# Token tile 1 before the samples in the later norms, its first two query blocks projected alone

## The chip, the cores and the metric

The kernel runs on one core of one Trainium2 chip, in one launch. The metric is the device time of that launch in microseconds (us), the median of three executions. All arithmetic is fp32.

## The reference

One layer of a decoder trunk, for 512 prompt tokens and 8 sample tokens of width 1024. The first half (windowed attention, gated DeltaNet, two gates, an output projection) yields `x`. The second half is a retrieval of single experts, and it is the stage that the change touches:

```python
mix = merged @ p['w_out']
x = x + gt1 * _rmsnorm(mix, p['g_post_mix'])
h2 = _rmsnorm(x, p['g_pre_ffn']) * (1.0 + sc2) + sh2
# _peer(h2, w_query, sub_keys, expert_u, expert_v), for each token and each of 8 heads:
qry = (xb @ w_query)                     # 16 blocks of 128 columns, two for each head
s = einsum(qry, sub_keys)                # two score rows of 128 keys for each head
sv, si = top_k(s, 16)                    # then the best 16 of the 16 x 16 sums
u, v = expert_u[eidx], expert_v[eidx]    # 16 rows of each, 1024 wide
out += (gate * gelu(xb . u)) * v
x = x + gt2 * _rmsnorm(out, p['g_post_ffn'])
```

## The kernel before

**Tiles and units.** The tokens are four tiles of 128 (t = 0 to 3) and the 8 samples (t = NT = 4). The expert stage is a list of 33 units (tile, head), eight for each tile and one for the samples. A unit of a token tile has 8 ticks, and there are 260 ticks. In each tick GpSimd issues two gathers (L480), each of 128 rows of 2048 floats (an expert's u and v side by side, 1.05 MB) into a ring of 7 slots. So tick i owns gathers 2i and 2i + 1, and units change at ticks 8, 16, 24 and so on. Tile 1 begins at tick 64.

**The ring.** For each gather VectorE makes a dot product with the tile's activations (L2390), ScalarE applies Gelu (L890) and makes a diagonal of weights (L892), and TensorE multiplies by the v half into `fsum` or `dbank` (L1648, L1654) and frees the slot. GpSimd may issue gather n only when TensorE is done with gather n - 7. Every engine works through its own program in order.

**What is woven in.** While tile 0's units run, the engines also finish the first half for the later tiles, and this work stands at fixed ticks, in tables written by hand: the remaining gates (`GATE_AT`), tile 0's query blocks (`FIRST_AT`), the output projection of the later tiles in four quarters e of three ticks each (`MIX_FROM`, `mixes_at`), the two norms (`NORMAL`, `SECOND`), the transposition of `h2` (`TURN`), then the 16 query blocks of all later tiles and the samples (`QUERY`, TOK - P = 392 columns at once). `SPREAD` broadcasts vectors of the modulation over the partitions. The keys of these tables are ticks. `LATER` says in which order tiles go through mixes, norms and TURN. In `woven(i)` TensorE issues what belongs to tick i, after the tick's two expert products; ScalarE empties the PSUM banks of tick i after the Gelus of tick i + 1; VectorE does its share at the end of tick i. Most of the woven products go through two PSUM banks (`abank0`, `abank1`) in turn.

**A query block.** It is 8 matmuls over `h2T[1]`, half of them before the first expert product of the next tick (`query_begin`) and half behind it (`query_end`). TensorE first waits until `h2T_ready` is NT + 1 = 5: tile 0, the samples and tiles 1 to 3 are all turned. ScalarE counts `h2T_ready` up at the end of each `turned`. Scores for the first head of tile 1 need blocks 0 and 1 (`scores(1, "first")`), and VectorE searches them at the end of tick 55, behind a wait for `first_sc`. The weights of a block (512 KB) come by SyncE's queue into four places; the load of a block waits until the block four before it has been used.

**The full rows of h2.** `second_part(t, None)` on VectorE rewrites tile t's `h2` for the dot products, at the ticks in `ROWS_LATER`, behind a wait for `h2T_ready`. In the kernel before tile 1's waits only for its own turn (3), tile 2's for 4, tile 3's for 5.

## Time and profile before

| | |
|---|---|
| median of 3 executions | 1865.48 us (1865.09 to 1865.55) |
| the profiled execution | 1861.27 us, its span 1859.5 us |
| TensorE | 1447.3 us busy, 78% of the span |
| VectorE, ScalarE, GpSimd | 67%, 38%, 33% |
| bytes moved | 647.54 MB, 348 GB/s over the span |

The table of the page divides the span into 40 slices of 46.5 us. The first gather is issued at 461.9 us; from slice 11 on (465 us) the DMA engines are nearly always busy and carry most of the time. In slices 15 to 20 the rate falls below that of the slices around them. A share of busy time is a mean over the whole span, and stages with different limits lie in it.

### The profile page before, as it was taken

To read this page: it belongs to the slowest core of one execution; us is meant where nothing else is said; L and a number is where in the kernel's file an instruction comes from. 1 tells how busy PE (TensorE), PEld (TensorE's weight loads), DVE (VectorE), ACT (ScalarE), POOL (GpSimd) and SP (SyncE) were. 2 spreads that over 40 slices of the span, in tenths; PEclk is the share of its full clock that TensorE was granted. 3 is DMA by queue.
4 is the path that set the end of the run, shared out by engine and by line. 5 is a ranking of instruction groups with operands and counts; after the bars stand their busy time and mean duration, and the time that the engine had idled before them with its cause. 6 is when DMAs were issued, how large, how long until landed. Compare 5 with 4: busy or idle time off the path is not lost.

```text
span 1859.5 us, 23227 instructions
## 1 busy us (share of the span) xinstructions
PE 1447.3 (78%) x8298; PEld 684.0 (37%) x8298; DVE 1248.9 (67%) x2827; ACT 704.1 (38%) x1799; POOL 611.3 (33%) x590
## 2 busy tenths in 40 slices
PE   8999988999888889689776666666666676667666
PEld 4777877887454446444222111101111110001001
DVE  3077678776866665776767666777667677667665
ACT  3145472213545553935324222432222243222223
POOL 1100000000543323333445444454444444444442
PEclk9999998999999999899988767867766676665666
DMA  9533362126999999999999999999999999999997
GB/s 348 179 121 118 129 241 80 35 80 219 417 421 419 422 414 405 401 342 394 413 420 423 425 424 424 425 424 425 424 424 423 421 423 417 422 421 418 423 422 305
DMA packets 101059, 647.54 MB, mean 348 GB/s; under 512 B 11858, under 2 KB 12026, under 8 KB 32933
## 3 DMA queue, kind: packets, MB, share of 16 engines
q0 software_dynamic: 76912, 555.82, 72.3%
q1 hardware_dynamic: 23840, 90.16, 13.3%
q8 instruction: 66, 1.08, 0.2%
q14 instruction: 49, 0.40, 0.1%
q10 hardware_dynamic: 192, 0.09, 0.0%
HBM read 640.84 MB, written 6.18 MB: 348 GB/s over the span
## 4 chain that ended last, share of the span: by engine, by line
PE 38%; DMA 38%; DVE 9%; ACT 9%; issue 5%; POOL 1%; ACTq 0%; SPq 0%; DVEq 0%; POOLq 0%
DMA arena<-in_euv,consts 37%; PE abank L926 23%; PE dbank L1654 4%; PE dbank L926 4%; DVE arena L2390 3%; PE fsum L1654 2%; PE fsum L1648 2%; ACT consts L892 2%; ACT L890 2%; ACT small L890 1%; ACT L795 1%; DMA arena<-in_wstream 1%; PE fsum L990 1%; POOL arena L480 1%; PE abank L1538 1%
## 5 line engine op out<-in xcount | busy, mean ns | idle before, releaser
L2390 DVE CUSTOM_DVE_ANT_0 arena<-arena 128x1024 f32<-128x1024 f32 x520 | 632.8, 1223 | 387.6 <-DMA arena<-in_euv,consts 386.7
L480 POOL DMA_INDIRECT arena<-in_euv,consts x520 | 577.0, 1110 | 784.3 <-PE dbank L1654 335.5
L926 PE MATMUL abank<-arena 128*128 128x128 f32 (+4 forms) x2456 | 555.1, 383 | 19.5 <-ACT arena L497 6.9
L1654 PE MATMUL dbank<-arena,consts 128*32 128x512 f32 x1024 | 364.5, 850 | 202.2 <-ACT consts L892 201.9
L926 PEld LDWEIGHTS abank<-arena 128*128 128x128 f32 (+1 forms) x2456 | 393.0, 191 | 176.0 <-issue 65.4
L890 ACT ACTIVATE small<-small 128x1 f32<-128x1 f32 x520 | 104.7, 201 | 639.5 <-DVE small L2390 632.9
L1654 PE MATMUL fsum<-arena,consts 128*32 128x512 f32 x512 | 191.2, 873 | 113.9 <-ACT consts L892 113.3
L1654 PEld LDWEIGHTS dbank<-arena,consts 128*32 128x32 f32 x1024 | 42.4, 124 | 487.9 <-ACT consts L892 475.9
L497 ACT ACTIVATE arena<-abank 128x512 f32<-128x512 f32 (+5 forms) x237 | 116.0, 489 | 253.2 <-PE abank L926 240.0
L892 ACT ACTIVATE consts<-arena,small 128x32 f32<-128x32 f32 x520 | 167.1, 321 | 16.9
L1654 PEld LDWEIGHTS fsum<-arena,consts 128*32 128x32 f32 x512 | 21.6, 126 | 263.5 <-ACT consts L892 261.0
L1648 PE MATMUL fsum<-arena,consts 128*32 128x256 f32 x1024 | 77.3, 410 | 41.1 <-ACT consts L892 40.9
L926 PE MATMUL dbank<-arena 128*128 128x128 f32 (+6 forms) x544 | 79.7, 315 | 0.4 <-DVEq L1817 0.4
L890 ACT ACT_TABLE_LOAD x57 | 73.1, 1283 | 4.2 <-DVE small L2390 1.8
L926 PEld LDWEIGHTS dbank<-arena 128*128 128x128 f32 (+2 forms) x544 | 67.0, 201 | 9.6 <-issue 4.6
L1648 PEld LDWEIGHTS fsum<-arena,consts 128*32 128x32 f32 x1024 | 25.1, 112 | 89.5 <-ACT consts L892 59.1
L459 POOL DMA_DIRECT2D out_deltas<-arena x1 | 0.5, 539 | 145.4 <-DVEq L2020 145.4
L497 ACT ACT_TABLE_LOAD x27 | 34.6, 1283 | 22.8 <-PE abank L926 21.7
L2390 DVE DVE_READ_ACCUMULATOR2_ANT small<- 128x1 f32 x520 | 42.8, 82 | 0.0
L795 ACT ACT_TABLE_LOAD x32 | 41.1, 1283 | 1.5
L2256 DVE MAX8 arena<-arena 128x8 f32<-128x128 f32 (+3 forms) x99 | 30.0, 331 | 15.7 <-ACTq L780 7.7
L1553 PE MATMUL abank<-arena,consts 128*32 128x512 f32 x256 | 39.6, 692 | 0.9 <-ACT arena L773 0.9
(338 smaller groups left out, 1196.1 us busy)
## 6 DMA issues: line engine op xcount, KB each, us to landing
arena<-in_wstream SPq DMA_DIRECT2D x140, 512.0 KB, 6.2
arena<-in_euv,consts POOLq DMA_INDIRECT x520, 13.2
arena<-in_wout SPq DMA_DIRECT2D x8, 1024.0 KB, 8.8
arena<-in_x SPq DMA_DIRECT2D x5, 512.0 KB, 6.8
arena<-in_sdel POOLq DMA_DIRECT2D x1, 2048.0 KB, 9.1
out_deltas<-arena POOLq DMA_DIRECT2D x1, 2048.0 KB, 12.0
out_yp<-arena SPq DMA_DIRECT2D x4, 512.0 KB
arena<-mod SPq DMA_DIRECT2D x3, 512.0 KB, 10.0
```

The costliest lines, as they stand in the source:

```text
L480: pool.indirect_dma_start(ring[n % SLOTS], None, I["euv"], bass.IndirectOffsetOnAxis(cur[:, u % 2, c:c + 1], 0)).then_inc(ring_in[n % SLOT ...
L497: step(A(dst, src, func, **kw), s.aring_free)
L795: A(gexp[r, :], best[r, :], ACT.Exp, bias=nbest[r, :], accum_out=gsum[r, :]).then_inc(s.gexp_ready, 1)
L890: step(A(gel[:, q % 2, place:place + 1], dot[:, q % 2, place:place + 1], ACT.Gelu), s.gelu_done)
L892: A(S[:, q % 2, place, :], E4g[:, u % 2, c0:c0 + 32], ACT.Copy, scale=gel[:, q % 2, place:place + 1]).then_inc(s.diag_ready, 1)
L926: return pe.matmul(out, lhsT, rhs, start=first, stop=last)
L990: last = pe.matmul(mod_bank[0][32 * j:32 * j + NCOND, half * 256:half * 256 + 256], cT[:, at_, :], w[:, j * 256:(j + 1) * 256], start=at_ ...
L1553: last = pe.matmul(b[32 * k:32 * k + 32, :], ident[:, 32 * j:32 * j + 32], h2_all[t][:, g * 512:(g + 1) * 512], start=True, stop=True, ski ...
L1648: last = pe.matmul(out[bank][32 * strip:32 * strip + 32, 256 * (e % 2):256 * (e % 2) + 256], weighed, v, start=first, stop=h == PH - 1 and ...
L1654: last = pe.matmul(out[e][to:to + 32, :], weighed, v, start=h == 0 and kk == 0, stop=h == PH - 1 and kk == 3, skip_group_check=True)
L2256: did(key, dve.max(val[:, 0:8], src))
L2390: TTR(uh, uh, rep[j] if t < NT else h2sb, 1.0, 0.0, ALU.mult, ALU.add, dot[:, n // NQ % 2, n % NQ:n % NQ + 1]).then_inc(s.dots_done, 1)
```

## The change

Tile 1 goes first through mixes, norms and TURN. `MIX_FROM` is one tick later, and with it all mixes; the gates from the tenth on stand up to one tick later and tile 0's last query block one tick sooner. The norms and turns are two ticks later. The first two query blocks of tile 1 alone (128 columns) are projected at ticks 51 and 52 (`ALONE`); their other 264 columns follow at ticks 76 and 79, for which their weights are loaded a second time. The other blocks run from tick 54 on. The last `SPREAD` moves from tick 56 to tick 63.

```diff
-        LATER = [NT, 1, 2, 3]
+        LATER = [1, NT, 2, 3]
...
-        MIX_FROM = 34
+        MIX_FROM = 35
...
-        NORMAL = {45: 0, 46: 1, 47: 2, 48: 3}
-        SECOND = {47: 0, 48: 1, 49: 2, 50: 3}
-        TURN = {48: 0, 49: 1, 50: 2, 51: 3}
-        ROWS_LATER = {53: 1, 55: 2, 57: 3}
-        QUERY_AT = (52, 53, 54, 55, 57, 58, 59, 62, 64, 67, 70, 73, 76, 79, 82, 85)
...
+        NORMAL = {47: 0, 48: 1, 49: 2, 50: 3}
+        SECOND = {49: 0, 50: 1, 51: 2, 52: 3}
+        TURN = {50: 0, 51: 1, 52: 2, 53: 3}
+        ROWS_LATER = {54: 1, 56: 2, 58: 3}
+        ALONE = {51: 0, 52: 1}
+        QUERY_AT = (54, 55, 57, 58, 59, 62, 65, 68, 71, 74, 76, 79, 83, 86, 89, 92)
+        QUERY = dict(zip(QUERY_AT, list(range(2, 12)) + [0, 1] + list(range(12, 2 * PH))))
...
-        SPREAD = {36: (0, 1), 39: (2, 3), 42: (4, 5), 44: (8,), 56: (6, 7)}
+        SPREAD = {37: (0, 1), 40: (2, 3), 43: (4, 5), 47: (8,), 63: (6, 7)}
...
+                if i in ALONE:
+                    pe.wait_ge(s.h2T_ready, 2)
+                    project(h2T[1], ((0, P),))
...
+                lo = P if m < 2 else 0
...
-            for n in range(N_AGAIN + 4, N_AGAIN + B_QRY):
+            for n in range(N_AGAIN + 4, N_AGAIN + B_QRY + 2):
...
                 if i in ROWS_LATER:
-                    dve.wait_ge(s.h2T_ready, ROWS_LATER[i] + 2)
+                    dve.wait_ge(s.h2T_ready, NT + 1)
                     second_part(ROWS_LATER[i], None)
```

TensorE around the last turn. In the kernel before: the turn of tile 3 (four matmuls for each half), tick 52's expert products, and then query block 0 on 392 columns.

```order
L926 MATMUL abank<-arena 128x128 [waits aring_free,h2_ready]
L926 MATMUL abank<-arena 128x128 x3
L926 MATMUL abank<-arena 128x128 [waits aring_free]
L926 MATMUL abank<-arena 128x128 x3
L1648 MATMUL fsum<-arena,consts 32x256 [waits diag_ready]
L1648 MATMUL fsum<-arena,consts 32x256 x3
L1648 MATMUL fsum<-arena,consts 32x256 [waits diag_ready]
L1648 MATMUL fsum<-arena,consts 32x256 x3
L926 MATMUL abank<-arena 128x392 [waits aring_free,w_full0,h2T_ready]
L926 MATMUL abank<-arena 128x392 x3
```

And in the changed kernel, from the second block alone (tick 52) to the turn of tile 3 (tick 53):

```order
L932 MATMUL abank<-arena 128x128 [waits aring_free,w_full1,h2T_ready]
L932 MATMUL abank<-arena 128x128 x7
L1665 MATMUL fsum<-arena,consts 32x256 [waits diag_ready]
L1665 MATMUL fsum<-arena,consts 32x256 x3
L1665 MATMUL fsum<-arena,consts 32x256 [waits diag_ready]
L1665 MATMUL fsum<-arena,consts 32x256 x3
L932 MATMUL abank<-skt,arena 128x128 [waits aring_free,qry_ready]
L932 MATMUL abank<-skt,arena 128x128
L932 MATMUL abank<-arena 128x128 [waits aring_free,h2_ready]
L932 MATMUL abank<-arena 128x128 x3
L932 MATMUL abank<-arena 128x128 [waits aring_free]
L932 MATMUL abank<-arena 128x128 x3
```

The blocks of 128 columns and the first scores (from `skt`) now stand ahead of the last turn, and the first block of 392 columns comes two ticks later than before.

VectorE at ticks 53 to 55. The pairs on L2390 are the dot products of the ring, L2172 and L2173 the full rows of tile 1, and L2256 the search of tile 1's first scores. Before:

```order
L2330 TENSOR_TENSOR arena<-consts 128x512 [waits diag_ready,egs_ready]
L2172 SCALAR_TENSOR_TENSOR arena<-arena,small 128x1024 [waits h2T_ready]
L2173 TENSOR_TENSOR arena<-arena 128x1024 [waits dve_step]
L2390 ISA arena,small<-arena 128x1024 [waits ring_in3,h2_ready]
L2390 ISA small 128x1
L2390 ISA arena,small<-arena 128x1024 [waits ring_in4]
L2390 ISA small 128x1
L2390 ISA arena,small<-arena 128x1024 [waits ring_in5]
L2390 ISA small 128x1
L2390 ISA arena,small<-arena 128x1024 [waits ring_in6]
L2390 ISA small 128x1
L2256 MAX arena<-arena 128x8 [waits eg_ready,first_sc]
```

In the changed kernel:

```order
L2347 TENSOR_TENSOR arena<-consts 128x512 [waits diag_ready,egs_ready]
L2407 ISA arena,small<-arena 128x1024 [waits ring_in3]
L2407 ISA small 128x1
L2407 ISA arena,small<-arena 128x1024 [waits ring_in4]
L2407 ISA small 128x1
L2189 SCALAR_TENSOR_TENSOR arena<-arena,small 128x1024 [waits h2T_ready]
L2190 TENSOR_TENSOR arena<-arena 128x1024 [waits dve_step]
L2407 ISA arena,small<-arena 128x1024 [waits ring_in5,h2_ready]
L2407 ISA small 128x1
L2407 ISA arena,small<-arena 128x1024 [waits ring_in6]
L2407 ISA small 128x1
L2273 MAX arena<-arena 128x8 [waits eg_ready,first_sc]
```

Tile 1's rows moved behind the dot products of tick 54, and their wait is now for the value 5, which comes with the turn of tile 3. The search stays at tick 55.

ScalarE in the second norms. Each row on L675 is a sum of squares, followed by a table load and a square root. Before, around `NORMAL`'s last tile, with the samples' turn (128x8x8) between the root and the next Gelu:

```order
L675 ACTIVATE arena,small<-arena 128x1024
L676 ACT_TABLE_LOAD
L676 ACTIVATE small<-small 128x1
L497 ACTIVATE arena<-abank 128x8x8
L890 ACT_TABLE_LOAD
L890 ACTIVATE small<-small 128x1
L892 ACTIVATE consts<-arena,small 128x32
```

In the changed kernel at the same place (128x128 x8 is the turn of tile 1):

```order
L677 ACTIVATE arena,small<-arena 128x1024
L678 ACT_TABLE_LOAD
L678 ACTIVATE small<-small 128x1
L764 ACTIVATE arena<-abank,small 128x128 x8
L896 ACT_TABLE_LOAD
L896 ACTIVATE small<-small 128x1
L898 ACTIVATE consts<-arena,small 128x32
```

The turn of tile 1 now shares a tick with the last of the norms.

## Rows read from the trace of the kernel before

**Rows 1.** The page: the span, the rate in its 40 slices, the chain.

```profile
span 1859.5 us, 23227 instructions
...
GB/s 348 179 121 118 129 241 80 35 80 219 417 421 419 422 414 405 401 342 394 413 420 423 425 424 424 425 424 425 424 424 423 421 423 417 422 421 418 423 422 305
...
PE 38%; DMA 38%; DVE 9%; ACT 9%; issue 5%; POOL 1%; ACTq 0%; SPq 0%; DVEq 0%; POOLq 0%
```

**Rows 2.** Windows: start:end, length, busy us of each engine, PEclk, DMA share, GB/s.

```profile
680.00:740.00 60.00, 52.30 (x515) 39.43 (x516) 34.25 (x86) 22.64 (x69) 20.34 (x19) 0.91 0.99 402
740.00:795.00 55.00, 35.22 (x368) 23.63 (x367) 40.01 (x66) 50.76 (x110) 21.66 (x21) 0.84 1.00 406
795.00:850.00 55.00, 51.10 (x264) 25.11 (x264) 40.23 (x106) 17.29 (x55) 17.36 (x16) 0.94 0.91 343
850.00:900.00 50.00, 42.47 (x272) 17.59 (x272) 34.21 (x82) 29.86 (x78) 21.60 (x20) 0.93 0.99 403
900.00:1000.00 100.00, 76.43 (x374) 28.39 (x368) 64.49 (x160) 31.68 (x103) 45.56 (x43) 0.95 1.01 419
1000.00:1400.00 400.00, 259.25 (x1080) 47.41 (x1080) 282.36 (x695) 128.03 (x392) 182.42 (x171) 0.72 1.01 424
```

**Rows 3.** Two windows inside 795:850, same columns.

```profile
820.00:830.00 10.00, 7.16 (x36) 3.94 (x28) 9.38 (x22) 5.45 (x12) 1.89 (x2) 0.90 0.95 376
830.00:840.00 10.00, 10.00 (x46) 4.43 (x48) 9.93 (x32) 1.77 (x6) 3.18 (x3) 0.76 0.63 226
```

**Rows 4.** Waits from 790 to 870 us: total us, times, longest.

```profile
POOL arena L480 <- PE fsum L1648: 46.3, 19, 6.7
...
DVE arena L2256 <- ACTq L780: 7.7, 1, 7.7
```

**Rows 5.** Timeline of TensorE: start us, length us, what, idle before it.

```profile
708.53 3.72 PE L926 MATMUL abank<-arena 128*128 128x256 f32 x16
...
790.79 1.16 PE L926 MATMUL abank<-arena 128*128 128x128 f32 x8 [0.74 <-ACT arena L762]
...
795.74 2.90 PE L926 MATMUL abank<-arena 128*128 128x392 f32 x8 [2.79 <-ACTq L764]
798.57 0.64 PE L1648 MATMUL fsum<-arena,consts 128*32 128x256 f32 x8
...
828.41 2.07 PE L926 MATMUL abank<-onehot,consts 16*128 16x256 f32 x4 [2.57 <-ACT arena L497]
...
832.28 4.16 PE L926 MATMUL abank<-arena 128*128 128x392 f32 x8
...
846.92 0.64 PE L1648 MATMUL fsum<-arena,consts 128*32 128x256 f32 x8
```

**Rows 6.** Timeline of ScalarE, same columns.

```profile
791.77 3.88 ACT L762 ACTIVATE arena<-abank,small 128x128 f32<-128x128 f32 x8
795.76 0.20 ACT L890 ACTIVATE small<-small 128x1 f32<-128x1 f32 x1
796.00 0.32 ACT L892 ACTIVATE consts<-arena,small 128x32 f32<-128x32 f32 x1
...
825.79 1.28 ACT L890 ACT_TABLE_LOAD   x1
```

**Rows 7.** ScalarE's groups from 740 to 800 us: count, busy us, mean ns.

```profile
L676 ACT ACT_TABLE_LOAD x6 | 7.7, 1283 | 0.1
```

**Rows 8.** Timeline of VectorE: a dot, the full rows, the search.

```profile
795.36 1.22 DVE L2173 TENSOR_TENSOR arena<-arena 128x1024 f32<-128x1024 f32 x1
...
799.68 1.23 DVE L2390 CUSTOM_DVE_ANT_0 arena<-arena 128x1024 f32<-128x1024 f32 x1 [0.69 <-DMA arena<-in_euv,consts]
...
811.06 0.49 DVE L2256 MAX8 arena<-arena 128x8 f32<-128x128 f32 x2 [7.68 <-ACTq L780]
```

**Rows 9.** DMA issues: KB of each, median us to landing.

```profile
arena<-in_wstream SPq DMA_DIRECT2D x140, 512.0 KB, 6.2
arena<-in_euv,consts POOLq DMA_INDIRECT x520, 13.2
```

More of the change, by code:

```diff
@@ L330, in scores_at @@
                 return 0, FIRST_AT[i - 1] // 4
-            if QUERY.get(i - 1) == 1:
+            if ALONE.get(i - 1) == 1:
                 return 1, "first"
@@ L337, in scores_at @@
             return None
+        SCORED = [(0, 0), (0, 1)] + [x for x in map(scores_at, range(len(TICKS))) if x and x[1] != "first"]
         LATE = unit_of(1, 0)
@@ L846, in woven @@
                     turned(LATER[TURN[i]])
+                if i in ALONE:
+                    empty(qryL[0][:, ALONE[i], 0:P], slice(0, P))
+                    act.sem_inc(s.qry_ready, 1)
                 if i in QUERY:
@@ L1488, in first_query, with asked_at, query_begin @@
                 project(h2T[0], ((0, P),))
+            def asked_at(t, m):
+                if t == 0 or t == 1 and m < 2:
+                    return m + 1 + (2 * PH if t else 0)
+                return 2 * PH + 3 + list(QUERY.values()).index(m)
             begun = [None, None]
-            def query_begin():
+            def query_begin(m):
+                lo = P if m < 2 else 0
                 w, b = weights(), aring.to_fill()
                 for k in range(KT // 2):
-                    last = mm(b[:, 0:TOK - P], w[:, k, :], h2T[1][:, k, :], k == 0, False)
+                    last = mm(b[:, lo:TOK - P], w[:, k, :], h2T[1][:, k, lo:], k == 0, False)
                     if k == 0:
@@ L1498, in query_begin, with query_end @@
                 begun[0], begun[1] = w, b
-            def query_end():
+            def query_end(m):
+                lo = P if m < 2 else 0
                 w, b = begun
                 for k in range(KT // 2, KT):
-                    last = mm(b[:, 0:TOK - P], w[:, k, :], h2T[1][:, k, :], False, k == KT - 1)
+                    last = mm(b[:, lo:TOK - P], w[:, k, :], h2T[1][:, k, lo:], False, k == KT - 1)
                 last.then_inc(s.aring_full, 1)
@@ L1516, in scores @@
                 g = 0 if g == "first" else g
-                pe.wait_ge(s.qry_ready, 4 * g + max(part) + 1 + (2 * PH if t else 0))
+                pe.wait_ge(s.qry_ready, max(asked_at(t, 4 * g + x) for x in part))
                 b = aring.to_fill()
@@ L1591, in woven @@
                     turned(LATER[TURN[i]])
+                if i in ALONE:
+                    pe.wait_ge(s.h2T_ready, 2)
+                    project(h2T[1], ((0, P),))
                 if i in QUERY:
                     pe.wait_ge(s.h2T_ready, NT + 1)
-                    query_begin()
+                    query_begin(QUERY[i])
                     if replicated(i):
-                        query_end()
+                        query_end(QUERY[i])
                 if replicated(i):
```

19 lines of the change are left out of this document (9 added, 10 removed).

## The prediction

> **What bounds the kernel now.** I read the page first. The chain that ended last is shared equally by TensorE and DMA, 38% each, and the row of rates says where each rules: from slice 21 on the rate stands near 424 GB/s, in slices 14 to 20 it falls to 342 to 414 [rows 1]. So the kernel is bound by bytes wherever the ring is kept fed, and time can be won only where the DMA engines run below 424 GB/s, or by moving fewer bytes. I then cut that part into windows and turned each rate into idle DMA time, length x (424 - rate) / 424: 3.1 us in 680:740, 2.3 in 740:795, 10.5 in 795:850, 2.5 in 850:900, 1.2 in 900:1000 and none in 1000:1400 [rows 2]. That is 19.6 us, over half of it in 55 us, and there TensorE is 93% busy (51.1 of 55). At 740:795 it is ScalarE instead, 50.8 of 55.
>
> Third, I counted gathers in the timelines to put ticks on these times (the dot at 799.68 us is number 110, the first of tick 55). 795:850 holds ticks 53 to 59, and so the query blocks 0 to 6. Half a block takes 2.90 us and the next product starts 2.83 behind it; two halves and two products come to 6.8 us for a tick [rows 5]. The bytes of such a tick need less: a gather has 1.05 MB, 2.47 us at 424 GB/s, a block 0.52 MB, 1.24 us [rows 9], together 6.2 us. TensorE therefore paces the ring, GpSimd waits for it 19 times, 46.3 us in all [rows 4], and ever fewer gathers are in flight. The deepest dip comes behind one event: at 828.41 TensorE has waited 2.57 us for ScalarE, the clock is granted at 0.76 over the next window, which is a stretch at 1.2 GHz and the rest at 2.4, half a block takes 4.16 us instead of 2.90, and the rate is 226 GB/s [rows 3, 5]. In the same ten ticks VectorE waits 7.7 us for the first scores [rows 4, 8], but the indices of tile 1 are not late; it costs only what it holds back of the ring.
>
> **The change, part by part.** *Bytes.* Two blocks are loaded twice: 2 x 1.24 = **+2.5 us**, in a stretch where DMA is the bound and nothing covers it. All other loads only move.
>
> *Start.* Everything from the mixes on stands one tick later, so one more tick of gathers goes ahead of it: 2 x 2.47 = 4.9 us later on the clock, with the same bytes moved per tick, no gain and no loss. Gates move by at most a tick in a stretch with hardly any idle time: nothing.
>
> *Norms, ticks 44 to 54.* ScalarE's list grows. Before, the last mean of the mixes and the first of the second norms fell into the same tick and shared one pair of table loads; now they are in two ticks: 2 x 1.28 = 2.6 us [rows 7]. The stretch has one more tick, with two Gelus and two diagonals at 0.20 + 0.32 each [rows 6], 1.0 us. Emptying two banks of 128 columns and the first scores' bank I put at 0.9 us, from 0.3 us each. Together +4.5 us, so the end of the last turn, at 791.77 + 3.88 = 795.65 us before [rows 6], comes 9.4 us later, but with gather 109 used and not 105. TensorE has room for the two blocks alone (2.3 us each, twice the 1.16 us of 8 records [rows 5]), since it is idle for 20 of 55 us there [rows 2]. In bytes this stretch needs 4 gathers and 2 blocks more, 12.4 us, against 9.4 us of time: about 0.8 us of its 2.3 us of idle DMA is filled, the rest of the difference makes the ring shallower.
>
> The Trainium skill would have this dearer: its page "ScalarE: Activation LUTs", section "What ACT_TABLE_LOAD costs", gives 1283 ns for a load plus about 1380 ns of drain, so 5.3 us for the added pair. The trace agrees with the first part, 1283 ns [rows 7], and not with the second: six loads have 0.1 us of idle time ahead of them together. By the page the sum below would be up to 2.7 us worse.
>
> *Queries, from the last turn to the product of gather 119 (tick 59).* Before: 795.65 to 846.92 + 0.64 = 847.56, 51.9 us [rows 5, 6]. Now blocks 2 to 5 stand in between and not 0 to 5 with part of 6. I lay out the new order with the durations of before. VectorE now waits at tick 54 for the last turn (value 5). Behind that wait stand the full rows of tile 1, the dots of tick 55 and the search; ScalarE's Gelus and TensorE's product 110 wait for those. Two passes at 1.22, a dot at 1.23, Gelu and diagonal 0.5: product 110 can start 4.2 us behind the turn [rows 6, 8]. TensorE has half a block to do meanwhile, 2.9 us, so it loses 1.3. Then: 8 halves at 2.83 = 22.7, 10 products at 0.57 = 5.7, scores and selection 1.1. At tick 57 ScalarE still has the exponential of tile 1's first unit, with two table loads, ahead of its Gelus, and I let the 2.57 us wait stand, and the slow clock behind it: a product and a half block at half speed, 2.2 us. The sum is 1.3 + 22.7 + 5.7 + 1.1 + 2.6 + 2.2 = 35.6 us, 16.3 less than before. With the turn 9.4 us later, product 119 ends **6.9 us sooner**, with the same gathers and blocks fetched. This much idle DMA time is filled at least by TensorE's pace. It can be more, as the ring is fuller at that point: in those 35.6 us DMA could bring 12 gathers and 5 blocks, 35.8 us, so it would hardly stop. The ends are 4 us (the first 1.3 us grows to 4 when gather 110 is late) and 12.8 us (all of 740:850). I take 7.8, with the 0.8 of above in it, since the layout by rows is the nearer of the two.
>
> *Behind it.* The last SPREAD goes from tick 56 to 63, where the scores use a bank too: three banks in one tick, of which TensorE has two, as in tick 56 before. At tick 63 TensorE was late and ScalarE ahead, so I take 1.0 us for its two products and not the dip; the ends are 0 and 5.8 us (the idle time of both windows [rows 3]). The other columns of blocks 0 and 1, at ticks 76 and 79: 264 columns take about the 3.72 us of 256 [rows 5], where a tick has room; ticks with a block at 900:1000 leave 1.2 us idle for six blocks, so two more 0.3 us.
>
> **Sum.** +2.5 - 7.8 + 1.0 + 0.3 = **-4.0 us**. The profiled execution, 1861.27 us with a span of 1859.5 [rows 1], would come to 1857.3. It lies 4.2 us under the median of the runs, so the same difference put on the median gives 1865.48 - 4.0 = **1861.5 us**. A measurement of this kernel tells about 0.2%, 3.7 us, from no change; the forecast lies at that edge.
>
> **The rivals.** *A, the ring stays fed.* With both blocks out of the way, in-flight gathers never run out, and of the 12.8 us nearly all is filled: -12 + 2.5 + 1.3 = -8 us, 1857 us. For it: the byte count of 35.8 against 35.6 us. Against it: the wait of 2.6 us and the slow clock are still in the order.
>
> *B, the new wait gives it back.* VectorE's wait for the value 5 holds the dots of ticks 55 and 56 until ScalarE has done the last turn, and the ring, shallower now, empties there as it did behind the wait of 7.7 us [rows 8]. The gain falls to 4: -4 + 3.8 = about 0, 1865.5 us. For it: in the old order the last turn was behind VectorE's dots of tick 53 only for tile 3's rows, and there was slack; now there is none. Against it: TensorE waits for the same turn anyway.
>
> *C, slower: the spread at the tile's change.* At tick 63 TensorE needs a third bank, which ScalarE empties only after the Gelus of tick 64, and these wait for the first dots of tile 1. If TensorE stands still there, the clock falls for the replicas and the block that follow. Price: a second dip like that of 820:840, 5.8 us, while the first stays where it is (tick 57) and eats 3.9 of the 7.8: +2.5 - 3.9 + 5.8 + 0.3 = +4.7, 1870.2 us. It decides once TensorE idles over 2.5 us at tick 63 or 64. Against it: in the old order ScalarE had emptied ahead of TensorE at this tick.
>
> *D, the stretch isn't paced by the blocks:* only the second load counts, +2.5 us, 1868. The windows speak against it.
>
> **The numbers.** The forecast 0.40, A 0.17, B 0.23, C 0.12, D 0.08. The forecast's own range is 1859.5 to 1864, so it is half above and half below the bound of 3.7 us. Faster by over 0.2%: 0.22 of the forecast, A, and a little of B's low side, 0.42. Slower by over 0.2%: C and some of D, 0.14. Within: 0.44. The range runs from A's lower half to D, 1856.5 to 1868.5, and leaves out C and the tail of A.
>
> **What would show it.** Right: the product of gather 119 ends near 841 us, the window 795:850 carries 370 to 400 GB/s, the turn of tile 3 ends near 805 us, 1.28 us loads stay two to a tick of the norms, and the row of rates is flat at 424 from 900 us on with two more blocks in it. Wrong: a wait of VectorE for ScalarE over 6 us at tick 54 with a rate under 300 behind it (B); TensorE idle over 2.5 us near tick 64 (C); slices 17 and 18 unchanged (D). A turn that ends later than 808 us would make the prediction too low, since all behind it hangs on its time.

## The result, and the profile after

The changed kernel takes 1877.38 us (8 runs), the kernel before 1864.57 us beside it: ratio 1.0071, 95% interval 1.0052 to 1.0089, 13.2 us slower (0.0071 x 1864.57). The forecast was 4 us faster. A second set of runs (c0 below) gave 1.0091 (1.0065 to 1.0116). Its page, of an execution of 1877.11 us, with the rows that answer to [rows 1]:

```profile
span 1875.3 us, 23300 instructions
...
GB/s 360 167 131 105 126 263 54 35 108 234 420 421 420 421 398 382 362 343 384 372 422 422 423 424 425 424 424 425 422 424 424 419 416 408 424 424 424 418 424 314
DMA packets 101348, 648.59 MB, mean 346 GB/s; under 512 B 11891, under 2 KB 12059, under 8 KB 33222
...
PE 42%; DMA 32%; DVE 9%; ACT 9%; issue 5%; POOL 1%; another core or an unknown queue 1%; ACTq 0%; SPq 0%; DVEq 0%; POOLq 0%
```

The chain that ended last leans more on TensorE now (42%, 38% before) and less on DMA (32%, 38% before). The windows of [rows 2], now:

```profile
680.00:740.00 60.00, 53.06 (x501) 37.60 (x500) 31.25 (x82) 20.22 (x63) 16.23 (x19) 0.86 0.96 379
740.00:795.00 55.00, 37.26 (x342) 24.80 (x340) 37.46 (x60) 41.41 (x86) 21.89 (x19) 0.81 0.94 367
795.00:850.00 55.00, 42.34 (x289) 24.83 (x290) 37.82 (x94) 27.70 (x75) 17.35 (x17) 0.91 0.90 354
850.00:900.00 50.00, 41.87 (x264) 17.86 (x263) 29.72 (x83) 25.19 (x66) 18.38 (x17) 0.90 0.92 360
900.00:1000.00 100.00, 77.67 (x332) 27.91 (x332) 66.89 (x157) 34.36 (x107) 46.88 (x43) 0.86 1.00 412
```

Idle DMA time by the prediction's formula, length x (424 - rate) / 424, is 6.4, 7.4, 9.1, 7.5 and 2.8 us, against 3.1, 2.3, 10.5, 2.5 and 1.2 before. The stretch that was to gain, 795:850, gained 1.4; those around it lost 15.0.

To follow the loss tick by tick, I take as the end of tick k the end of its second diagonal on ScalarE (L892 before, L898 after). The changed kernel is behind by 6.9 us at tick 59 (849.3 against 842.4), 5.7 at tick 62, 13.3 at tick 68 (905.7 against 892.4), 15.0 at tick 100 and 15.8 at the end. So there are two losses: one ahead of tick 59, where a gain was forecast, and 7.6 us from tick 62 to 68, around the change to tile 1.

**The first loss.** ScalarE and TensorE at the turns. ScalarE first:

```profile
793.36 1.04 ACT L677 ACTIVATE arena<-arena 128x1024 f32<-128x1024 f32 x1
...
794.51 1.28 ACT L678 ACT_TABLE_LOAD   x1
...
796.14 3.90 ACT L764 ACTIVATE arena<-abank,small 128x128 f32<-128x128 f32 x8
800.13 1.28 ACT L896 ACT_TABLE_LOAD   x1
...
813.60 3.90 ACT L764 ACTIVATE arena<-abank,small 128x128 f32<-128x128 f32 x8 [0.45 <-PE abank L932]
```

TensorE:

```profile
793.06 1.08 PE L1665 MATMUL fsum<-arena,consts 128*32 128x256 f32 x16
798.21 0.63 PE L1479 MATMUL abank<-consts,arena 8*128 8x8 f32 x8 [4.07 <-ACT arena L764]
800.17 3.75 PE L932 MATMUL abank<-arena 128*128 128x128 f32 x16 [1.34 <-ACTq L766]
803.86 1.94 PE L1665 MATMUL fsum<-arena,consts 128*32 128x256 f32 x16
...
817.59 2.90 PE L932 MATMUL abank<-arena 128*128 128x392 f32 x8 [2.14 <-ACTq L766]
822.02 0.64 PE L1665 MATMUL fsum<-arena,consts 128*32 128x256 f32 x8 [1.53 <-ACT consts L898]
...
836.75 1.93 PE L1665 MATMUL fsum<-arena,consts 128*32 128x256 f32 x16 [2.91 <-ACT consts L898]
838.62 3.52 PE L932 MATMUL abank<-arena 128*128 128x392 f32 x8
...
852.62 0.64 PE L1665 MATMUL fsum<-arena,consts 128*32 128x256 f32 x8
```

The last mean with its table load, tile 1's whole turn and the load back for Gelu now lie between the Gelus of two ticks; TensorE waits 4.07 us, then its work takes nearly twice as long (3.75 us for 16 records that take 1.95 at 812.50). This wait is easy to see, but it is a small part of the loss: with the short tick behind it, ticks 52 and 53 take 9.0 + 2.9 us, where ticks 50 and 51 took 5.3 + 4.9 before. By the ends of the ticks, the two kernels are only 0.6 us apart at tick 45. Tick 46 takes 11.3 us instead of 5.7, ticks 47 to 51 take the same (27.7 and 27.5 us), the two added ticks take the 11.9 us, and the last turn ends 12.1 us behind its tick instead of 8.7. In tick 46 ScalarE first waits for a mix on TensorE, then has two means, a root for each, the emptying of the samples' mix in four pieces and a pair of table loads ahead of its Gelus:

```profile
757.69 0.38 ACT L499 ACTIVATE arena<-abank 128x256 f32<-128x256 f32 x1 [3.15 <-PE abank L932]
...
763.56 1.28 ACT L896 ACT_TABLE_LOAD   x1
```

The last turn ends at 813.60 + 3.90 = 817.50, product 119 at 852.62 + 0.64 = 853.26.

**The second loss.** TensorE at the tile change. First the kernel before (L1553 are the replicas of ticks 64 and 65, L1654 the products, the 5.53 us are query block 8 at tick 64):

```profile
871.12 5.53 PE L926 MATMUL abank<-arena 128*128 128x392 f32 x16
876.58 1.06 PE L1553 MATMUL abank<-arena,consts 128*32 128x512 f32 x8
878.55 1.07 PE L1553 MATMUL abank<-arena,consts 128*32 128x512 f32 x8 [0.90 <-ACT arena L773]
879.43 1.04 PE L1654 MATMUL dbank<-arena,consts 128*32 128x512 f32 x8
880.29 1.90 PE L1553 MATMUL abank<-arena,consts 128*32 128x512 f32 x16
```

The changed one, with the block at tick 65:

```profile
877.44 1.94 PE L1671 MATMUL dbank<-arena,consts 128*32 128x512 f32 x8
879.15 0.61 PE L1552 MATMUL abank<-arena,consts 128*32 128x8 f32 x32
879.60 2.51 PE L1567 MATMUL abank<-arena,consts 128*32 128x512 f32 x16
885.95 2.37 PE L1671 MATMUL dbank<-arena,consts 128*32 128x512 f32 x8 [3.84 <-ACT consts L898]
888.25 6.93 PE L932 MATMUL abank<-arena 128*128 128x392 f32 x16
895.11 1.93 PE L1567 MATMUL abank<-arena,consts 128*32 128x512 f32 x16
```

And ScalarE in the same microseconds: it empties the sums of tile 0's heads, and the next Gelus stand behind.

```profile
880.85 4.46 ACT L745 ACTIVATE arena<-fsum 128x256 f32<-128x256 f32 x11 [0.18 <-ACT consts L499]
```

In the kernel before, the same emptying runs from 872.27 to 876.73 us, and TensorE computes block 8 beside it (871.12 to 876.65):

```profile
872.27 4.46 ACT L743 ACTIVATE arena<-fsum 128x256 f32<-128x256 f32 x11 [0.17 <-ACT consts L497]
```

Now TensorE waits 3.84 us, and the block comes behind the wait and takes 6.93 us instead of 5.53; the granted clock is 0.63 in 883:888 and 0.69 in 888:893, so part of it ran at the lower level.

### The profile page after: what moved, and what is told of

Same layout as the page of the kernel before. It is cut to its first block, busy times and chain, and to the rows that moved or that the text cites. A ratio compares the mean times of both kernels' runs of the same rounds, so it can differ in the third digit from the quotient of the medians.

```text
span 1875.3 us, 23300 instructions
## 1 busy us (share of the span) xinstructions
PE 1432.8 (76%) x8330; PEld 687.8 (37%) x8330; DVE 1249.4 (67%) x2827; ACT 703.3 (38%) x1802; POOL 617.5 (33%) x590
## 2 busy tenths in 40 slices
DMA packets 101348, 648.59 MB, mean 346 GB/s; under 512 B 11891, under 2 KB 12059, under 8 KB 33222
## 3 DMA queue, kind: packets, MB, share of 16 engines
q1 hardware_dynamic: 24128, 91.20, 13.2%
q8 instruction: 66, 1.08, 0.2%
## 4 chain that ended last, share of the span: by engine, by line
PE 42%; DMA 32%; DVE 9%; ACT 9%; issue 5%; POOL 1%; another core or an unknown queue 1%; ACTq 0%; SPq 0%; DVEq 0%; POOLq 0%
DMA arena<-in_euv,consts 32%; PE abank L932 25%; PE dbank L1671 4%; PE dbank L932 4%; DVE arena L2407 3%; PE fsum L1665 2%; PE fsum L1671 2%; ACT consts L898 2%; ACT L896 2%; PE abank L1552 1%; ACT small L896 1%; POOL arena L482 1%; ACT L798 1%; PE fsum L996 1%; DMA arena<-in_wstream 1%
## 5 line engine op out<-in xcount | busy, mean ns | idle before, releaser
L482 POOL DMA_INDIRECT arena<-in_euv,consts x520 | 583.1, 1121 | 796.0 <-PE dbank L1671 337.8
L932 PE MATMUL abank<-arena 128*128 128x128 f32 (+4 forms) x2488 | 562.7, 384 | 20.8 <-DVE arena L1963 5.4
L1671 PE MATMUL dbank<-arena,consts 128*32 128x512 f32 x1024 | 351.0, 857 | 216.5 <-ACT consts L898 215.8
L932 PEld LDWEIGHTS abank<-arena 128*128 128x128 f32 (+1 forms) x2488 | 402.0, 194 | 183.3 <-issue 70.0
L499 ACT ACTIVATE arena<-abank 128x512 f32<-128x512 f32 (+6 forms) x239 | 116.5, 487 | 260.8 <-PE abank L932 248.0
L898 ACT ACTIVATE consts<-arena,small 128x32 f32<-128x32 f32 x520 | 167.1, 321 | 16.9
L896 ACT ACT_TABLE_LOAD x57 | 73.1, 1283 | 4.1 <-DVE small L2407 1.8
L499 ACT ACT_TABLE_LOAD x27 | 34.6, 1283 | 38.9 <-PE abank L932 37.8
L798 ACT ACT_TABLE_LOAD x32 | 41.1, 1283 | 1.4
L499 ACT ACTIVATE consts<-abank 128x32 f32<-128x32 f32 (+1 forms) x33 | 6.5, 197 | 92.4 <-PE abank L1552 75.1
## 6 DMA issues: line engine op xcount, KB each, us to landing
out_deltas<-arena POOLq DMA_DIRECT2D x1, 2048.0 KB, 11.4
```

Of the source, the lines that this page charges most:

```text
L482: pool.indirect_dma_start(ring[n % SLOTS], None, I["euv"], bass.IndirectOffsetOnAxis(cur[:, u % 2, c:c + 1], 0)).then_inc(ring_in[n % SLOT ...
L499: step(A(dst, src, func, **kw), s.aring_free)
L798: A(gexp[r, :], best[r, :], ACT.Exp, bias=nbest[r, :], accum_out=gsum[r, :]).then_inc(s.gexp_ready, 1)
L896: step(A(gel[:, q % 2, place:place + 1], dot[:, q % 2, place:place + 1], ACT.Gelu), s.gelu_done)
L898: A(S[:, q % 2, place, :], E4g[:, u % 2, c0:c0 + 32], ACT.Copy, scale=gel[:, q % 2, place:place + 1]).then_inc(s.diag_ready, 1)
L932: return pe.matmul(out, lhsT, rhs, start=first, stop=last)
```

## The experiments

Ratios are to the kernel before, run beside each variant on the same chip, with 95% intervals. Runs whose names start with e or c edit the changed kernel, those with b the kernel before. The other columns are of one profile each: the end of the last turn, the end of tick 59, the time from the end of tick 62 to the end of tick 68, idle DMA time in 740:850 and 850:900, all in us.

| run | edit | ratio | turn | tick 59 | 62 to 68 | idle |
|---|---|---|---|---|---|---|
| before | | | 795.6 | 842.4 | 31.5 | 12.8, 2.6 |
| after | | 1.0071 [52, 89] | 817.5 | 849.3 | 39.1 | 16.5, 7.6 |
| c0 | after again | 1.0091 [65, 116] | 813.8 | 845.6 | 42.2 | 16.0, 10.9 |
| e1 | own turn's wait | 1.0038 [22, 55] | 811.9 | 843.7 | 37.2 | 14.1, 7.4 |
| e2 | spread at 56 | 1.0046 [31, 61] | 811.7 | 846.7 | 36.7 | 17.4, 6.6 |
| e3 | block 8 at 64 | 1.0016 [-2, 34] | 810.5 | 842.4 | 33.1 | 15.2, 3.3 |
| e4 | mixes at 34 | 1.0019 [5, 33] | 808.6 | 840.5 | 37.2 | 12.7, 7.9 |
| b1 | before, block 8 at 65 | 1.0030 [19, 42] | 798.4 | 847.7 | 39.6 | 15.9, 9.3 |
| b2 | before, tile 1 first | 1.0012 [-3, 27] | 797.2 | 846.9 | 33.4 | 18.7, 6.3 |
| e5 | e3 + e4 | 1.0011 [2, 21] | 805.0 | 837.5 | 35.7 | 13.1, 6.2 |
| e6 | block 8 at 66 | 1.0043 [26, 61] | 813.9 | 845.7 | 37.8 | 15.8, 5.5 |
| e7 | e3, alone at 52, 53 | 1.0030 [16, 44] | 816.0 | 847.3 | 35.7 | 14.9, 7.7 |
| e8 | e3 + e1 | 1.0034 [20, 48] | 821.0 | 851.4 | 35.7 | 14.7, 7.2 |
| e9 | all two ticks sooner | 1.0002 [-8, 13] | 796.0 | 833.0 | 40.3 | 10.6, 7.7 |
| e10 | useless work at 64 | 1.0062 [36, 88] | 820.7 | 852.6 | 39.7 | 16.7, 6.4 |
| e11 | e9, block 8 at 64 | 0.9991 [-24, +6] | 799.0 | 835.5 | 37.3 | 12.1, 6.0 |
| e12 | e11, alone at 51, 52 | 0.9987 [-29, +4] | 796.1 | 833.4 | 36.5 | 11.4, 2.6 |
| c1 | e3 again | 1.0023 [9, 37] | 817.0 | 848.8 | 34.3 | 16.7, 5.2 |
| b3 | before, spread at 63 | 1.0003 [-7, 13] | 795.2 | 841.6 | 36.0 | 12.4, 6.4 |
| e13 | e12, spread at 59 | 0.9976 [-36, -12] | 798.6 | 833.5 | 34.8 | 9.9, 5.5 |

(Brackets: the interval's distance from 1 in units of 0.0001.)

### First group: one part undone at a time

The three theories: N, the norms and mixes at later ticks; W, VectorE's new wait at tick 54; T, the tile change. Edits of the changed kernel (e1, e2, e3, e4):

```diff
-                    dve.wait_ge(s.h2T_ready, NT + 1)
+                    dve.wait_ge(s.h2T_ready, {1: 2, 2: 4, 3: 5}[ROWS_LATER[i]])
...
-        SPREAD = {..., 63: (6, 7)}
+        SPREAD = {..., 56: (6, 7)}
...
-        QUERY_AT = (54, 55, 57, 58, 59, 62, 65, 68,
+        QUERY_AT = (54, 55, 57, 58, 59, 62, 64, 68,
...
-        MIX_FROM = 35
+        MIX_FROM = 34
```

(e4 also takes back the gates, first queries and the first four spreads by up to three ticks.)

> The changed kernel, but each of VectorE's full-row passes waits only for its own tile's turn (h2T_ready 2, 4, 5 at ticks 54, 56, 58) and not for the last. Theory W (the wait): in the trace of the changed kernel VectorE stands 12.2 us at tick 54 and the rate falls to 264 GB/s behind it (800:810), so this gives back 4 to 8 us. Theory N (the norms): the turn of tile 3 ends at 817.5 us, 21.9 us later than before with only two ticks more done, and TensorE's first block of 392 columns waits for the same turn, so it gives 0 to 2 us. Theory T (the tile's change at ticks 63 to 67): 0.

> The changed kernel with the last SPREAD back at tick 56. Theory T in its form of rival C (the three banks at tick 63): the idle DMA time of 880:910, 7.6 us, goes, 4 to 7 us faster, less what the spread costs at tick 56, up to 3. Theories W and N: the spread at tick 63 took 2 us of TensorE and no stall, so 0, or 1 to 3 us slower by the stall at tick 56 that comes back.

> The changed kernel with query block 8 at tick 64 and not 65, as in the kernel before. Theory T in its second form: at tick 64 a block lies beside ScalarE's emptying of the tile's sums and VectorE's pass over them, at tick 65 it stands in line behind them together with two replicas, on a cold TensorE (6.93 us for the block): 3 to 6 us faster, and the idle time of 880:910 falls from 7.6 to 3. Theories W and N: 0.

> The changed kernel with gates, tile 0's query blocks, mixes and the first spreads at the ticks of the kernel before (mixes from 34, spreads at 36, 39, 42, 44); norms, turns and blocks stay as changed. Theory N: of the 12.5 us by which the last turn came later than forecast, about 4 are in the mixes, where the exponential of tick 44 now falls into the tick whose spread TensorE waits for; they come back, 4 to 7 us faster, and the turn of tile 3 ends near 812. Theories W and T: the wait and the tile's change stay, 0 to 2 us.

In the changed kernel VectorE waits 12.17 us for the last turn:

```profile
817.57 1.28 DVE L2189 SCALAR_TENSOR_TENSOR arena<-arena,small 128x1024 f32<-128x1024 f32 x1 [12.17 <-ACTq L766]
```

In e1 that wait is gone, and yet from the last turn to tick 59 both kernels take 31.8 us (849.3 - 817.5, 843.7 - 811.9): TensorE waits for the same turn anyway. e2 pays for its spread between the ends of ticks 54 and 59 (40.0 us against 36.8) and gets some of it back at tick 65 (7.9 against 10.8). e3 brought most with one number, e4 nearly as much. All four came out nearer to the kernel before than either set of the changed one, so the four savings cannot simply be added. T forecast 3 to 6 us for e3; by the medians it came out 10 us nearer to the kernel before (1.0071 to 1.0016).

### Second group: transplants into the kernel before

> The changed kernel once more, unedited, on the chip of this call. It tells how much of the difference between it and its variants is the kernel's own scatter. The profiled execution shown first had its last turn at 817.5 us and idle DMA time of 6.4 us in 680:740; the four variants, which don't touch that stretch (three of them), had the turn at 810.5 to 811.9 and 2.9 to 3.1 (one 1.7). Theory S (scatter: the 5 us extra of the mixes belong to that one execution): last turn at 810 to 812, about 1871 us, ratio to the kernel before 1.004 to 1.005. Theory K (the extra 5 us are the kernel's own): last turn over 815 us, about 1876 us, ratio 1.007.

> The kernel BEFORE with one entry changed: query block 8 at tick 65 instead of 64, nothing else (tile 1 last but two as before, spread at 56). Theory T (the tile change is what costs: block 8 at tick 65 meets two replicas, its half block waits for a bank and runs at the slow clock): 3 to 6 us slower than before, idle DMA time in 850:900 from 2.6 to 6 or more, block 8 over 5 us on TensorE. Rival T2 (it costs only together with the spread at tick 63 and the ring made shallow by the norms): within 1 us of before.

> The kernel BEFORE with the order of the changed one alone: tile 1 goes through mixes, norms and turns ahead of the samples; nothing else moves, no block is projected alone, each tile's full rows wait only for that tile's turn. Theory O (the order itself costs: the mix of 128 columns, 3.7 us, stands where that of 8 samples was, so ScalarE's table loads and the exponential of tick 44 are waited for): last turn 2 to 5 us later than before, 2 to 4 us slower. Rival O2 (the order costs nothing; the blocks alone and the later ticks do): last turn within 1.5 us of before, time within 1 us of before.

> The changed kernel with both of the best edits: block 8 at tick 64 as before, and gates, first queries, mixes and the first four spreads at the ticks of the kernel before. Norms and turns stay at their new ticks, the blocks alone stay at 51 and 52. If the two costs are apart (mix ticks 3 to 5 us, tile change 5 to 7 us) it comes to about 1861 us, equal to the kernel before or 2 us under it, with the last turn at 808 us and idle DMA time of 3 to 4 us in 850:900. If the ring's depth at the tile change is what both act on (one cost seen twice), it stays at 1864 us.

c0 fits neither theory as put: its turn, 813.8, lies between the two, and its time is that of K. b1 is the cleanest experiment: one number, 64 to 65, in a kernel with nothing else changed, costs 5.6 us (0.0030 x 1864.09), and TensorE shows the same pattern, 4.15 us of waiting and a block of 6.88 us:

```profile
884.79 2.37 PE L1654 MATMUL dbank<-arena,consts 128*32 128x512 f32 x8 [4.15 <-ACT consts L892]
887.09 6.88 PE L926 MATMUL abank<-arena 128*128 128x392 f32 x16
```

The order alone (b2) is unclear at 1.0012; its last turn is 1.6 us later, nearer to O2. e5 (1.0011) is hardly better than e3 or e4 alone, so their gains don't add up.

### Third group: where the block may stand, and the ticks before

e6 puts 66 for 65 in `QUERY_AT`, e7 has `ALONE = {52: 0, 53: 1}`, e8 joins e1 and e3. e9 has everything sooner: it takes e4's tables and e1's waits, keeps the spread at 63, and sets:

```diff
+        NORMAL = {45: 0, 46: 1, 47: 2, 48: 3}
+        SECOND = {47: 0, 48: 1, 49: 2, 50: 3}
+        TURN = {48: 0, 49: 1, 50: 2, 51: 3}
+        ROWS_LATER = {53: 1, 55: 2, 57: 3}
+        ALONE = {50: 0, 51: 1}
+        QUERY_AT = (53, 54, 56, 58, 60, 62, 66, 68, 71, 74, 76, 79, 83, 86, 89, 92)
```

> The changed kernel with one entry changed: query block 8 at tick 66, one tick LATER than in the changed kernel, where no replica stands. Block 8 at tick 64 gained 13 to 14 us against the changed kernel run beside e5 (1864.0 against 1879.3, different calls), and moving it to 65 in the kernel before cost 5.7 us. Theory T (three banks at tick 65 - a whole block and two replicas behind each other - stop TensorE and bring it to the slow clock): tick 66 is as good as 64, 1862 to 1866 us, idle DMA time in 850:900 from 7.6-10.9 to under 4. Rival T3 (what helps is only that block 8 and the blocks behind it come sooner, so that one less stands in the ticks of tile 1): tick 66 is as bad as 65 or worse, over 1872 us.

> The changed kernel with block 8 at tick 64 (1864.0 us before) and the two blocks alone one tick later, at 52 and 53, so that the first of them no longer follows the turn of tile 1 by one tick and TensorE doesn't wait for ScalarE between two turns; the first scores come at tick 54 as in the kernel before. Theory A (TensorE's wait of 4.07 us ahead of the first block alone delays the turns): last turn from 810.5 to 805-807 us, idle DMA time in 740:795 from 5 to about 3, and 2 to 3 us faster than 1864 if nothing gives it back. Rival A2 (the first scores one tick later are waited for at tick 55, as in the kernel before, 7.7 us): the turn comes sooner but the time stays at 1863 to 1866.

> The changed kernel with block 8 at tick 64 and the full rows of each tile waiting for that tile's turn alone, as in the kernel before. Theory W (VectorE's wait of 12 us at tick 54 holds back the ring: idle DMA time of 5.2 us in 800:820): idle time there falls to 2 to 3, 2 to 3 us faster than 1864. Rival W2 (TensorE waits for the same turn, and the expert products for it: the wait alone moves nothing, as the path from the last turn to tick 59 was 31.8 us with and without it): within 1 us of 1864.

> The changed order (tile 1 first, its two blocks alone, their other columns late) with gates, mixes, norms and turns at the ticks of the kernel before, the blocks alone at 50 and 51, full rows waiting for their own tile's turn, the spread at 63, and query blocks 2 to 8 at 53, 54, 56, 58, 60, 62 and 66. It has all that the change was made of but its later ticks. If the later ticks and tick 65 were the whole loss: last turn near 800 us, idle DMA time of 6 us in 795:850 and 3 in 850:900, 1858 to 1861 us, under the kernel before. If the order and the blocks alone cost as much as they give (order alone: last turn +1.6 us, idle time +6.3 in 740:795): 1864 to 1867.

My theory T, three banks in one tick, fell with e6 as it was put: at tick 66 no replica stands, and ticks 62 to 68 still take 37.8 us, at 1872.4 us and not at 1862 to 1866 (its ratio, 1.0043, overlaps with that of the changed kernel). Over all profiles ticks 62 to 68 take 33.1 to 37.3 us in the variants with block 8 at 64, and 36.7 to 42.2 with it at 65 or 66; the two ranges touch. Theory A fell with e7: its last turn ends at 816.0 us and not at 805 to 807. Tick 52 takes 9.0 us with the first block alone at 51 or at 52, and in b2, which has no such block, tick 50 takes the same 9.0. What these kernels share is the order: the samples' small turn used to share a tick with the last mean, now tile 1's 3.9 us do. The next tick is shorter for it (1.2 us in e9, 4.9 before), which is why it costs little. e8 comes out no better than e3 and c1, as W2 had it, though not at W2's 1864 us. In e9 tick 59 ends at 833.0, but ticks 62 to 68 give 8.8 us of it back, with block 8 at 66. Its 1864.25 us are the time that was put for an order that costs as much as it gives, but tick 66 was changed with it, and e11 moves that.

### Fourth and fifth group: work for nothing, and the best version

e10 is the changed kernel, block 8 still at 65, with this in `replicate`, for tick 64 alone. The products are overwritten by the replica behind them:

```diff
+                    if (t, j, g) == (1, 2, 0):
+                        for k in range(KT):
+                            mm(b[:, 0:TOK - P], h2T[1][:, k, 0:P], h2T[1][:, k, :])
```

> The changed kernel plus work for nothing: at tick 64, ahead of the first replica of that tick, TensorE multiplies the 8 chunks of h2T by themselves into the bank that the replica then overwrites, 16 records of 392 columns, the size of one query block (5.5 us at full clock). Block 8 stays at tick 65 and nothing else moves. Theory F (block 8 at tick 64 was what TensorE did while ScalarE was busy with the sums of the next unit; without it TensorE stands idle 2.2 and 4.0 us between the replicas of ticks 64 and 65, the clock falls, and the block behind it takes 7.2 us instead of 5.5): with 5.5 us of useless work the kernel gets faster by 2 to 5 us, ratio to the kernel before 1.004 to 1.006, and the time from tick 62 to tick 68 falls from 39-42 us to 35-37. Rival T3 (the order of the blocks, one later each, is what costs): no gain or 3 to 5 us slower, ticks 62 to 68 over 40 us.

> Kernel e9 with query block 8 at tick 64 and not 66: ticks 62 to 68 took 40.3 us in e9, 31.4 in the kernel before, 33 to 36 in the variants with block 8 at 64. Theory F: ticks 62 to 68 in 33 to 36 us, 4 us faster than e9, ratio 0.997 to 0.999. If the ring's depth decides and not the block's place: same as e9, 1.000.

> Kernel e11 with the blocks alone at 51 and 52 in place of 50 and 51. In e9, whose norms are the same, tick 50 took 9.0 us since TensorE waited 3.2 us ahead of the first block alone, and idle DMA time was 9.4 us in 740:795. Theory A: tick 50 falls to 5 to 7 us, idle time there to 5 to 7, another 2 us faster than e11, ratio 0.996 to 0.998. Rival A2 (ScalarE's list of norms and turns sets these ticks, the block alone only fills): same as e11.

> The kernel of e3 once more on the chip of this call: block 8 at tick 64, all else as changed. e3 gave 1.0016 [0.9998, 1.0034], but e7 and e8, which add one more edit each, gave 1.0030 and 1.0034. If these edits did harm: 1.001 to 1.002 again. If e3 was a good draw: 1.003.

TensorE in e10, the useless work first:

```profile
883.71 5.53 PE L932 MATMUL abank<-arena 128*128 128x392 f32 x16
889.18 1.92 PE L1570 MATMUL abank<-arena,consts 128*32 128x512 f32 x16
892.16 1.50 PE L1674 MATMUL dbank<-arena,consts 128*32 128x512 f32 x8 [1.06 <-ACT consts L898]
893.59 5.53 PE L932 MATMUL abank<-arena 128*128 128x392 f32 x16
```

And windows of c0 and of e10 at this place (the third figure from the end is the granted clock):

```profile
878.00:883.00 5.00, 1.23 (x8) 0.16 (x8) 0.24 (x2) 2.88 (x9) 0.94 (x1) 0.77 0.98 393
883.00:888.00 5.00, 2.81 (x9) 0.88 (x10) 3.38 (x11) 3.59 (x10) 0.60 (x1) 0.50 0.40 162
888.00:893.00 5.00, 5.00 (x12) 2.59 (x11) 4.90 (x11) 1.05 (x4) 1.99 (x2) 0.70 0.68 234
```

```profile
885.00:890.00 5.00, 5.00 (x21) 2.38 (x23) 0.15 (x2) 2.92 (x9) 0.95 (x1) 1.00 1.00 403
890.00:895.00 5.00, 3.94 (x24) 1.28 (x17) 3.41 (x11) 3.56 (x11) 1.20 (x2) 1.00 0.37 151
895.00:900.00 5.00, 5.00 (x25) 2.33 (x27) 4.90 (x11) 1.72 (x6) 0.78 (x1) 1.00 0.98 356
```

5.53 us of extra work replace most of the waits (c0 has 2.16 and 4.00 us here, e10 has 1.06), the clock stays at 2.4 GHz (1.00 against 0.50, which is 1.2 GHz), and the real block takes 5.53 us and not 6.93 (7.25 in c0). The Trainium skill, page "TensorE: Matmul & The Clock Gate", Part 1, says that "the default state is throttled, and activity releases the throttle"; the two sets of windows agree, with 0.50 at the wait and 1.00 where work fills it.

The whole is not measurably dearer than the changed kernel (1.0062, intervals overlap), nor surely faster; 39.7 us for ticks 62 to 68 lies between 39.1 and 42.2, above the 35 to 37 of theory F. So no cost shows for 5.53 us of work at tick 64, as F has it, and the clock is kept; but F's gain doesn't show, so keeping the clock alone does not give what block 8 gives at tick 64. What is left is that its 5.5 us no longer stand at tick 65, behind the wait. That is an inference from e10, e3 and b1 together; no run shows it by itself.

Of the other three, e11 takes 37.3 us for ticks 62 to 68 against e9's 40.3, as F has it in direction, though above its 33 to 36; its 0.9991 can't be told from e9's 1.0002. In e12 tick 50 takes 9.0 us wherever the block alone stands, as A2 had it. c1 gives 1.0023, between its two forecasts.

The last two runs take e12's spread from 63 to 59 (e13), and move the spread alone in the kernel before (b3).

> Kernel e12 (the changed order with the norms and blocks two ticks sooner, block 8 at tick 64) with the last spread at tick 59, where neither a query block nor an exponential stands, and not at 63. In the traces tick 65 took 7.9 and 8.0 us with the spread at 56 (e2, the kernel before) and 9.5 to 12.1 us with it at 63. Theory P (the spread at 63 makes TensorE late for tick 64, so that the wait between the replicas comes later and the clock falls): tick 65 falls from 11.8 to 8 to 9.5 us, ticks 62 to 68 from 36.5 to 33, ratio to the kernel before 0.996 to 0.998, the first version surely faster than it. Rival P2 (tick 59 pays for it as tick 56 did, 3 us more in ticks 54 to 59): 0.9985 to 1.0, unclear against the kernel before.

> The kernel BEFORE with the last spread at tick 63 in place of 56, nothing else. The prediction put this at +1.0 us (ends 0 and 5.8) and took nothing for what its leaving tick 56 may give. From the traces: leaving tick 56 gives 3 us in ticks 54 to 59 (40.0 against 36.9), standing at 63 costs 1.5 to 4 us at tick 65. Theory P: ticks 54 to 59 from 38.5 to 36, tick 65 from 8.0 to 10 to 12, both together 0 to +3 us, ratio 1.000 to 1.0015. If the prediction's +1.0 holds for tick 63 and the gain at 56 is real: 1 to 2 us faster, 0.999.

e13 is 4.5 us faster than the kernel before (0.0024 x 1864.76), with an interval that leaves out no change: 1859.20 against 1864.76 us. Its windows:

```profile
740.00:795.00 55.00, 35.12 (x330) 24.29 (x330) 38.48 (x64) 47.37 (x103) 19.57 (x19) 0.75 0.93 366
795.00:850.00 55.00, 49.49 (x316) 25.85 (x320) 43.71 (x111) 21.03 (x65) 21.28 (x20) 0.94 0.98 405
```

795:850 carries 405 GB/s, where the kernel before had 343 [rows 2]. Of P, tick 65 fell (11.8 to 9.4 us), ticks 62 to 68 less than put (36.5 to 34.8). The step from e12 to e13 is within the intervals; that e13 beats the kernel before is measured. The spread at 59 was not tried in the kernel before, so how much of the 4.5 us is the spread's is not shown: without that move, e12 is unclear (0.9987, up to 1.0004).

In b3 the spread alone makes a wait at tick 64. TensorE stands 3.05 us between the two replicas, where it stood 0.90 before, and the products behind it take 1.95 us instead of 1.04:

```profile
880.70 1.24 PE L1553 MATMUL abank<-arena,consts 128*32 128x512 f32 x8 [3.05 <-ACT arena L773]
881.69 1.95 PE L1654 MATMUL dbank<-arena,consts 128*32 128x512 f32 x8
```

## Why the prediction was wrong

**What bounds the kernel: right.** Idle DMA time from 680 to 1000 us rose by 13.6 us (33.2 - 19.6) and the bytes by 2.5, together 16.1 us; the span rose by 15.8.

**Bytes, +2.5 us: agrees.** 648.59 - 647.54 = 1.05 MB more, 2.5 us at 424 GB/s. Past tick 68, where the second halves of blocks 0 and 1 stand (ticks 76 and 79), the changed kernel loses another 2.5 us (15.8 - 13.3); no run has the second loads alone. In 900:1000, where I put 0.3 us for the 264 columns, idle DMA time rose by 1.6 (2.8 - 1.2) in this one profile.

**Start and norms, last turn 9.4 us later: wrong, 21.9 us.** This is the first step that failed. In ten profiles of kernels with the new tables the last turn ends between 810.5 and 821.0 us, 815.4 in the mean, against my 805. The turns stand two ticks later. I priced the first of these ticks at the DMA time of its gathers, 4.9 us, and the second at its Gelus and diagonals alone, 1.0 us. The two added ticks take 11.9 us in the trace (9.0 + 2.9), as ScalarE has the last mean, a pair of loads and tile 1's whole turn in the first of them; 5.6 us more come at tick 46, and 3.4 us between the end of tick 53 and that of the turn. The prediction itself named a turn later than 808 us as the sign that it would be too low, and that sign came. The order and the blocks alone were not it: e9, e11, e12 and e13 have both, at the old ticks, and end the last turn at 796.0 to 799.0 (795.6 before). Between, with the mixes at the old ticks and the norms two later, lie e4 and e5, 808.6 and 805.0. So of the 18 us between the means of the two groups (815.4 and 797.4), about half goes with each of the two shifts, by two profiles. In time, e6 and e9, both with block 8 at 66, stand at 1.0043 and 1.0002 with intervals that don't touch: the later ticks cost 7.6 us, together with what else e9 sets otherwise (the waits, the blocks alone, the spacing of the blocks). The added pair of table loads, 2.6 us in the sum, is in the trace: seven loads for the roots where [rows 7] has six. ScalarE's loads once more have hardly any idle time ahead of them, by its groups from 740 to 815 us:

```profile
L896 ACT ACT_TABLE_LOAD x8 | 10.3, 1283 | 0.3
L678 ACT ACT_TABLE_LOAD x7 | 9.0, 1283 | 0.1
```

That is 0.4 us of idle time for 15 loads of 1283 ns; the drain of the page "ScalarE: Activation LUTs" of the Trainium skill ("What ACT_TABLE_LOAD costs") doesn't show.

**Queries, 35.6 us from the last turn to product 119: right, 35.8 us** (853.26 - 817.50), with its parts within 1 us each. TensorE's idle time behind the turn was put at 1.3 us and is 0.09 + 1.53 (the wait of 2.14 lies almost wholly before the turn's end); the wait of 2.57 us became 2.91; the slow clock was put at 2.2 us, and two products and a half block took 1.93 and 3.52 us instead of 1.08 and 2.90, 1.5 us more. But product 119 ended 5.7 us later than before and not 6.9 sooner, since the turn did not stand where I put it. Where the turns kept their ticks, it did come sooner, 839.94 + 0.64 = 840.58 us in e13:

```profile
839.94 0.64 PE L1665 MATMUL fsum<-arena,consts 128*32 128x256 f32 x8
```

That this is the forecast 841 is luck: there the turn ends at 798.65 and not at 805, and 41.9 us follow and not 35.6, since two more ticks lie behind the turn. The mechanism of the gain was right; the changed kernel paid more for its later ticks. (My 6.9 and 0.8 us make 7.7 and not 7.8, which changes nothing.)

**Spread, +1.0 us: right in number, by luck.** b3 gives +0.6 us, interval -1.3 to +2.4. But under it lie two larger effects, and my sum had neither. From the end of tick 54 to that of tick 59 the kernel takes 36.4 us instead of 38.5, since the spread has left; and tick 65 takes 12.0 instead of 8.0.

**The other blocks "only move": wrong, about 5 us.** This is the second step that failed. I gave block 8's step from tick 64 to 65 no price, and named no work that hid it. At tick 64 it lay beside ScalarE's 4.46 us of sums. b1 measures 5.6 us for it, interval 3.5 to 7.8. In the changed kernel it costs more by the medians: 1.0071 and 1.0091 with the block at 65, 1.0016 and 1.0023 with it at 64 (e3, c1), 9 to 14 us, though the intervals allow 3. What is left in e3 and c1, 3 to 4 us, is the price of the later turns less the gain of the queries.

**The rivals.** C had the right place and the right sign, and its sum, 1870.2 us, was the nearest. Its cause was not what is at work in the changed kernel: with the spread back at 56, e2 has the same wait ahead of block 8, 4.16 us, and b1, where it never moved, 4.15. But the wait that C describes exists: in b3 it is the 3.05 us at tick 64, though that kernel is only 0.6 us slower in all, not clear of nothing. B's wait was there, 12.17 us and over the 6 us that I named, with 264 GB/s in 800:810, but e1 shows that it does not lengthen the path from the turn to tick 59. A is contradicted by the windows of the changed kernel. D is contradicted by e13, where 795:850 carries 405 GB/s with fewer blocks in it; its sign, slices 17 and 18 unchanged, came by half (401 to 362, 342 to 343 GB/s).

**Open.** e1 and e2, with only the wait or the spread taken back, measured nearer to the kernel before than the changed one did, 1.0038 and 1.0046. Yet the wait's removal gave nothing on top of e3 (1.0034 with it, 1.0016 and 1.0023 without). The turns of e1 and e2 are 2 to 6 us sooner than those of the changed kernel, ahead of anything that these edits touch. The first group ran on another chip than the later ones: there e1, e2 and e3 end the last turn at 810.5 to 811.9 us and the kernel before takes 1861.17 us; the seven others with the new tables end it at 813.8 to 821.0, with the kernel before at 1864 to 1865. So part of this scatter may go with the chip; no run separates the two. Whether these two edits gain at all is not settled, nor why tick 46 takes 11.3 us in every kernel with the mixes at 35 and 5.7 to 7.3 with them at 34; what fills it is shown above, but no run moves the exponential of tick 44 or the last mix alone.

## What to carry to other kernels

A block of work that is moved "for free" may have been filling a wait: before moving it, look at what the other engines did beside it, and price what that wait is without cover. In an order written out in ticks, a delay costs ticks at the pace of that stretch, not the bytes in them. And when a change of many parts loses, undo its parts singly and transplant them singly: here the version with the idea (two blocks alone, fewer blocks ahead of the first scores), its old ticks put back and the spread at 59 is 4.5 us faster than the kernel before.
